# A decoder layer in fp32 on one core: the first norm's weights ride in with x, the other norm weights come later on GpSimd's queue, ten warm-up groups for twelve

## The reference, cut to what matters

```
h    = rmsnorm(x, attn_norm)                     # 16 x 128 weights: the first norm
proj = h @ w_in                                  # queries, keys, values of groups A and B
out_a = dilated_attention(...); out_b = swa_sink_attention(...)
mix  = concat(rmsnorm(out_a, out_norm_a), rmsnorm(out_b, out_norm_b))   # 8 + 8 columns
x    = x + mix @ w_out
h    = rmsnorm(x, ffn_norm)                      # 16 columns
x    = x + (silu(h @ w_gate) * (h @ w_up)) @ w_down
out  = rmsnorm(x, final_norm)
```

## Time and profile before

| | |
|---|---|
| median of 3 runs | 1980.23 us (1979.84 to 1980.58) |
| the profiled execution, whole | 1983.18 us |
| its span, first to last instruction | 1981.4 us |
| PE busy | 1968.1 us (99%) |
| DVE busy | 1654.0 us (83%) |
| ACT busy | 1124.8 us (57%) |
| POOL busy | 165.6 us (8%) |
| DMA, first of 40 slices | 9 tenths busy, 323 GB/s; mean over the span 139 GB/s |

### The profile page before, as it was taken

How to read it: one execution, slowest core, us unless ns; L and a number is a source line. 1 busy time by engine, 2 the same in 40 slices (tenths; PEclk the granted TensorE clock), 3 DMA queues, 4 the chain that set the end, 5 groups by cost and what they waited for, 6 DMA issues and landing times.

```text
span 1981.4 us, 29278 instructions
## 1 busy us (share of the span) xinstructions
PE 1968.1 (99%) x10300; PEld 1691.7 (85%) x10300; DVE 1654.0 (83%) x2384; ACT 1124.8 (57%) x2064; POOL 165.6 (8%) x261
## 2 busy tenths in 40 slices
PE   9999999999999999999999999999999999999998
PEld 7788888888888988888888888888888888888886
DVE  7877777767766999999999999999998688697886
ACT  6566666666446655555555555555556355566643
POOL 4002333323100000000000000000000000000000
PEclk9999999999999999999999999999999999999999
DMA  9422222223334344433434434444446846546433
GB/s 323 143 80 75 65 72 72 70 70 120 118 115 143 118 142 136 139 132 134 138 128 138 136 131 137 138 134 133 137 138 232 304 123 224 177 148 222 126 129 133
DMA packets 132745, 276.16 MB, mean 139 GB/s; under 512 B 13376, under 2 KB 13408, under 8 KB 131600
## 3 DMA queue, kind: packets, MB, share of 16 engines
q1 hardware_dynamic: 120752, 239.65, 37.8%
q0 software_dynamic: 6640, 23.82, 3.1%
q10 hardware_dynamic: 5232, 11.04, 1.6%
HBM read 242.99 MB, written 31.46 MB: 139 GB/s over the span
## 4 chain that ended last, share of the span: by engine, by line
PE 95%; DVE 2%; issue 1%; DMA 1%; ACT 0%; SPq 0%; POOLq 0%; POOL 0%; DVEq 0%; ACTq 0%
PE bank L835 25%; PE bank L838 13%; PE bank L762 7%; PE bank L764 7%; PE bank L763 7%; PE bank L696 7%; PE bank L698 7%; PE bank L697 7%; PE bank L894 3%; PE bank L892 3%; PE bank L893 3%; PE bank L919 2%; PE bank L936 1%; PE bank L904 1%; PE bank L903 1%
## 5 line engine op out<-in xcount | busy, mean ns | idle before, releaser
L835 PE MATMUL bank<-s_two,t_hi 128*128 128x512 f32 x2352 | 557.3, 390 | 0.0
L1479 ACT ACTIVATE t_hi<-t_raw 128x1792 fp32r<-128x1792 f32 x176 | 302.1, 1718 | 358.8 <-DVE t_raw L2149 272.0
L835 PEld LDWEIGHTS bank<-s_two,t_hi 128*128 128x128 f32 x2352 | 433.5, 188 | 84.7
L2155 DVE TENSOR_TENSOR t_lo<-t_raw,t_hi 128x1792 fp32r<-128x1792 f32 x176 | 355.3, 2019 | 22.0 <-ACT t_hi L1479 21.9
L838 PEld LDWEIGHTS bank<-s_two,t_lo 128*128 128x128 f32 x2352 | 298.8, 191 | 10.8 <-DVE t_lo L2155 1.0
L838 PE MATMUL bank<-s_two,t_lo 128*128 128x256 f32 x2352 | 302.1, 283 | 0.8 <-DVE t_lo L2155 0.8
L1130 ACT ACTIVATE w_hi<-raw 128x512 fp32r<-128x512 f32 x268 | 168.4, 629 | 191.5 <-PE bank L764 141.3
L1772 DVE TENSOR_TENSOR w_lo<-raw,w_hi 128x512 fp32r<-128x512 f32 x268 | 184.0, 688 | 58.0 <-ACT w_hi L1130 57.5
L2146 DVE TENSOR_TENSOR t_raw<-t_raw 128x1024 f32<-128x1024 f32 x176 | 214.7, 1220 | 16.7 <-DMA t_raw<-in_w_gu 14.5
L696 PE MATMUL bank<-h_hi,w_hi 128*128 128x512 f32 x416 | 166.1, 399 | 2.5 <-DVE w_lo L1772 1.9
L698 PE MATMUL bank<-h_lo,w_hi 128*128 128x512 f32 x416 | 162.6, 391 | 0.0
(11 more groups left out here) (257 smaller groups left out, 3483.6 us busy)
## 6 DMA issues: line engine op xcount, KB each, us to landing
t_raw<-in_w_gu SPq DMA_DIRECT2D x348, 256.0 KB, 2.8
raw<-in_w_down SPq DMA_DIRECT2D x112, 256.0 KB, 3.5
raw<-in_w_in SPq DMA_DIRECT2D x104, 256.0 KB, 2.7
gu_mid<-part POOLq DMA_DIRECT2D x43, 512.0 KB, 2.9
gu_next<-gu_mid SPq DMA_DIRECT2D x36, 512.0 KB, 6.5
raw<-in_w_out SPq DMA_DIRECT2D x64, 256.0 KB, 3.0
fast_y<-in_w_down SPq DMA_DIRECT2D x24, 512.0 KB, 5.0
fast_z<-in_w_down SPq DMA_DIRECT2D x16, 512.0 KB, 4.7
```

Of the source, the lines that this page charges most:

```text
L835: mm = nc.tensor.matmul(b[:, :], t_hi[r][:, ti, q, :], both, start=d == 0 and q == 0, stop=d == DOUBLES - 1 and q == 1 and i < 4, skip_gro ...
L1479: nc.scalar.activation(t_hi[r][:, :, :, :].rearrange("p a q c -> p (a q c)"), t_raw[r][:, 1:8, :, :].rearrange("p a q c -> p (a q c)"), AC ...
L2155: nc.vector.tensor_tensor(t_lo[r][:, :, :, :].rearrange("p a q c -> p (a q c)"), t_raw[r][:, 1:8, :, :].rearrange("p a q c -> p (a q c)"), ...
```

## The change

The sixteen columns of the first norm are put in front of the first block of x in HBM (`x_head`, 128 rows of 16 + 512 numbers), and the first DMA on SP's queue loads both into one stretch of each partition (`x_head_first`; `gain0` and `x_first` are views of it). `gains` keeps 32 columns; its load moves from ACT's first instruction to POOL's queue, behind `ident` and ahead of `band`. The three waits at the start of ACT, DVE and POOL go; DVE waits for `gains` before `neg_gain`, ACT before its first `act_high`. The warm-up has ten groups instead of twelve. `gains` is 64 bytes shorter in each partition and `gain0` takes 64 bytes ahead of `o_t`, so the tiles in between (`sink` to `h_lo`) stand 64 bytes lower, and so do the later tiles placed by them.

```diff
-WARM = 12
+WARM = 10
...
-    gains = sb("gains", [P, 2 * KD + 2 * PAIRS])
+    gains = sb("gains", [P, KD + 2 * PAIRS])
...
     h_lo = sb("h_lo", [P, KD, SEQ], F32R)
+    spot[0] += KD * BYTES
     place_o = spot[0]
...
-    x_first = sb("x_first", [P, KD, SEQ], at=place_o)
+    x_head_first = sb("x_head_first", [P, KD + KD * SEQ], at=place_o - KD * BYTES)
+    gain0 = x_head_first[:, 0:KD]
+    x_first = x_head_first[:, KD:KD + KD * SEQ].rearrange("p (k c) -> p k c", c=SEQ)
...
-    G_ATTN, G_FFN, G_OUT = 0, KD, 2 * KD
+    G_FFN, G_OUT = 0, KD
...
                 k0, k1 = X_PARTS[m]
+                if m == 0:
+                    sp.dma_start(x_head_first[:, 0:KD + SEQ], x_head).then_inc(x_loaded[0], 16)
+                    continue
...
-                                 scale=gains[:, G_ATTN + k:G_ATTN + k + 1]).then_inc(xt_hi_done, 1)
+                                 scale=gain0[:, k:k + 1]).then_inc(xt_hi_done, 1)
...
                 if p == PAIRS - 1 and s == 3:
+                    act.wait_ge(gains_loaded, 16)
                     act.wait_ge(kb_lo_done, 4)
...
-        act.dma_start(gains[:, :], gain_cols).then_inc(gains_loaded, 16)
         act.wait_ge(ones_done, 2)
         nc.scalar.activation(tick[:, 0:8], half[:, :], ACT.Copy, scale=half[:, 0:1]).then_inc(tables_loaded, 1)
-        act.wait_ge(gains_loaded, 16)
...
-            nc.vector.scalar_tensor_tensor(h_lo[:, k, :], x_first[:, k, :], gains[:, G_ATTN + k:G_ATTN + k + 1],
+            nc.vector.scalar_tensor_tensor(h_lo[:, k, :], x_first[:, k, :], gain0[:, k:k + 1],
...
                 if e == 39:
+                    dve.wait_ge(gains_loaded, 16)
...
-        dve.wait_ge(gains_loaded, 16)
...
-        pool.wait_ge(gains_loaded, 16)
...
-                nc.gpsimd.tensor_scalar(x_first[:, k, :], x_first[:, k, :], gains[:, G_ATTN + k:G_ATTN + k + 1], 1.0,
+                nc.gpsimd.tensor_scalar(x_first[:, k, :], x_first[:, k, :], gain0[:, k:k + 1], 1.0,
...
         nc.gpsimd.dma_start(ident[:, :], c_ident).then_inc(ident_loaded, 16)
+        nc.gpsimd.dma_start(gains[:, :], gain_cols).then_inc(gains_loaded, 16)
```

More of the change, by code:

```diff
@@ L128, with build @@
 HEAD = [("A", 0, 0), ("A", 1, 3), ("B", 0, 6), ("B", 1, 8)]
-def build(nc, x, x_turned, gain_cols, w_in, w_v, sinks, w_out, w_gu, w_down, final_norm, c_dist, c_lnm, c_band, c_slope, c_ident, x_mid, gu_mid, out):
+def build(nc, x, x_head, x_turned, gain_cols, w_in, w_v, sinks, w_out, w_gu, w_down, final_norm, c_dist, c_lnm, c_band, c_slope, c_ident, x_mid, gu_mid, out):
     spot = [(nc.sbuf_base + 63) // 64 * 64]
@@ L2635, in laid_out @@
     x, w_in = np.asarray(inputs["x"]), np.asarray(inputs["w_in"])
-    cols = [np.asarray(inputs[name])[0].reshape(-1, P).T for name in ("attn_norm", "ffn_norm", "out_norm_a", "out_norm_b")]
+    cols = [np.asarray(inputs[name])[0].reshape(-1, P).T for name in ("ffn_norm", "out_norm_a", "out_norm_b")]
+    gain0 = np.asarray(inputs["attn_norm"])[0].reshape(-1, P).T
+    x_head = np.concatenate([gain0, x[0].T[:P]], axis=1)
     w_v = w_in[0][:, 2 * D_A:3 * D_A]
@@ L2641, in laid_out @@
     w_gu = w_gu.transpose(4, 1, 0, 3, 2, 5).reshape(TILES, DOUBLES, 2, P, 4 * P)
-    return {"w_gu": np.ascontiguousarray(w_gu), "x_turned": np.ascontiguousarray(x[0].T), "gain_cols": np.ascontiguousarray(np.concatenate(cols, axis=1)),
+    return {"w_gu": np.ascontiguousarray(w_gu), "x_head": np.ascontiguousarray(x_head), "x_turned": np.ascontiguousarray(x[0].T), "gain_cols": np.ascontiguousarray(np.concatenate(cols, axis=1)),
             "w_in": np.ascontiguousarray(w_in), "w_v": np.ascontiguousarray(w_v)}
```

## The result

| | before | after |
|---|---|---|
| median of 6 runs each | 1980.67 us (1979.84 to 1982.77) | 1989.73 us (1988.95 to 1990.70) |
| profiled execution, span | 1981.4 us | 1988.8 us |
| ratio | | 1.0045 (95% interval 1.0035 to 1.0055) |

A forecast was written before the change was run, and what follows sets the result against it. SyncE's transfers were taken to bound 2 to 54 us, with TensorE 99% busy over the span. 0.10 us less before x's second row and 0.06 more before the fourth gave 0.04 less: 1980.2 us, range 1978.6 to 1982.0.

The forecast's parts named there:

- The step that failed: Tiles moved by 64 bytes: same shapes and operands for each instruction, so zero cost, with no row bounding it otherwise.
- the sign by which it would show: Forecast is wrong if TensorE's instructions from 60 us on take other times, because of the 64 bytes.
- The end moves only with the product at 54.26 us: From 54.26 us on TensorE waits for nothing of the head, so the end moves with that product alone.
- the 1927.1 us behind it: From the product at 54.26 us to the end: the same 1927.1 us expected after the change.
- The wait at 54.26: TensorE's 1.9 us wait, ending on x loads: expected again at another size, with 54.26 moved by less than 1.5 us.
- the second cover that I gave the head: What the head gains in compute is waited away at 39.80 and again at 54.26 us, where the wait was 1.9 us.
- `gains` out of the head: Start of the kernel: first `h_hi` at most 0.29 us earlier, first product 0.1 to 0.3 us earlier.
- The run's start: TensorE's unbroken run, starting at 7.59 us before, would start at about 7.5 us.
- The bytes on POOL's queue: The later `gains` load crosses x's fourth row: 0.06 us; rival, 1.1 us if it behaves like `sink`, chance 0.12.
- The warm-up: Two groups fewer before the first product: costs nothing and gives nothing; its 20 matmuls over by 5.3 us.
- The rival of the clock: Ten groups could put off the rise to 2.4 GHz; decides at 13.8 us at 1.2 GHz, 1984.2 us; chance 0.05.
- something unseen: Remaining case for any cause not named anywhere in the kernel; chance 0.03.

The follow-up runs named there:

- Experiment 2: Kernel before with only the small tile `sink` moved behind `h_lo`, so the tiles between stand 64 bytes lower: 1989.69 us, ratio 1.0046.
- experiment 4: Kernel after with `slope` and `sink` moved behind `h_lo`, so the low tiles stand 256 bytes lower than before against the rest: 1980.91 us, ratio 1.0002.
- experiment 6: Not the layer: bare products at seventeen pairs of operand offsets, other engines still; 512 columns took 226.7 ns at (0, 0), 233.3 at (64, 0).
- experiment 11: Not the layer: bare products again, in another order of blocks; short ones at 64 right behind products at distance 0 ran at 117.8 ns.
- experiment 1: Kernel before with ten warm-up groups instead of twelve and nothing else: 1980.52 us, ratio 1.0003.
- experiment 3: Kernel before with `sink` moved to the top of memory, every tile behind its old place 64 bytes lower, distances between large tiles kept: 1980.15 us, ratio 0.9998.
- experiment 7: The kernel of experiment 4 with twelve warm-up groups instead of ten: 1981.22 us, ratio 1.0002.
- experiment 10: The bare products of experiment 6 with both tiles 224 bytes higher: all seventeen pairs as there within 0.1 ns.

## Why the prediction was wrong, by its own steps

**The step that failed** is the shortest: "The tiles moved by 64 bytes: each instruction has the same shape and the same operands. Zero, and no row bounds it otherwise." That is the whole difference. Experiment 2 has only this and shows +9.1 us, experiment 4 has everything but this and shows +0.3, each against the kernel before on its own chip. I had named the sign by which it would show ("PE's instructions from 60 us on take other times") and had looked at no pair of tiles. The step could have been worked out as far as a question. In the kernel before, the large tiles lie multiples of 256 bytes apart, and so does each pair of them that PE multiplies; the change takes 64 from the tiles up to `h_lo` and leaves those from `o_t` on, so some pairs are no longer so. Which ones:

| products (512 columns if not said) | distance after, modulo 256 | before, ns | after, ns |
|---|---|---|---|
| `h_hi`, `w_hi`: both moved | 0 | 227 | 227 |
| `act_hi`, `w_hi`: the output projection, 530 to 590 us | 64 | 227 | 233 |
| `f_hi`, `a_hi`: down, 1620 to 1900 us | 64 | 226 | 233 |
| `w_hi`, `down_hi`, 1465 to 1550 us | 0 | 227 | 227 |
| `w_hi`, `down_hi`, 1620 to 1900 us, between `f` products | 0 | 226 | 232 |
| `s_two`, `t_hi`: gate and up, by slot | 0 or 64 | 228.2 | 229.8 |
| `s_two`, `t_lo` (256 columns), by slot | 0 or 64 | 120.1 | 118.3 |

Each line is a mean from start to start over the records of the group. The last two, 2352 products each, nearly cancel, 3.8 us lost and 4.0 gained. In the down projection the moving tile `f_hi` is the higher one; its products with `a_hi` and `a_lo` take 232.8 and 230.9 ns, more than the 228.9 of that side in experiment 6, which is there the pace of a long block once it has settled. The fifth was a riddle until experiment 11: these tiles both moved, yet they are slower only behind the `f` products. Split by their place there, the first twelve products behind an `f` product take 230.3 ns on average (500 of them), those further on 226.7 (144); before, all take 226.7. The excess lies in the first ten, as behind the bare (0, 64); the eleventh and twelfth take 226.7. That is 1.8 of the 5.4 us of this stretch: the slow pace outlasts its cause.

The profile's own mean durations hardly show it. The kernel after, by groups from 1620 to 1960 us (line, engine, operation, shapes and count | busy us, mean ns | idle):

```profile
L768 PE MATMUL bank<-w_hi,down_hi 128*128 128x512 f32 x248 | 97.7, 394 | 0.0
...
L769 PE MATMUL bank<-w_lo,down_hi 128*128 128x512 f32 x248 | 96.5, 389 | 0.0
```

Before, all such groups stand at 389. A mean of 394 for 389 ns, 1.3%, and no idle time: this is what nine microseconds look like.

**The end moves only with the product at 54.26 us.** True of the change's own work: that same product starts at 51.35 us in experiment 4 and at 51.27 and 51.32 in experiments 1 and 3, which have the head's loads of before. False of the end, since the 1927.1 us behind it, taken as fixed, grew by 10.0.

**The wait at 54.26.** Forecast to stay, at some other size. It was gone, and not by the change: ACT's fourth square started at 46.06 in the profiled execution of before; after, it reads

```profile
35.74 1.92 ACT L1372 ACTIVATE x_row<-x_row 128x2048 f32<-128x2048 f32 x1 [1.50 <-DMA x_row<-in_x]
...
43.19 1.90 ACT L1372 ACTIVATE x_row<-x_row 128x2048 f32<-128x2048 f32 x1
```

and experiments 1 and 3, whose loads are those of before, have it at 43.04 and 43.01. In the nine other profiled executions of the layer PE waits 0.3 us at this product once and otherwise not at all. The 1.9 us belonged to that one execution, which lay 2.95 us above the median; I had seen that and still took its waits for the kernel's. So the second cover that I gave the head, the wait behind 54 us, wasn't there. It did no harm to the sum: experiments 1, 4 and 7 show nothing gained or lost.

**`gains` out of the head**: the first `h_hi` 0.29 us earlier at most, measured 0.31; the first product 0.1 to 0.3, measured 0.40 (5.68 for 6.08); x0's load took 2.8 us for 2.9, so the rows of 2112 bytes cost nothing that shows. **The run's start**: 7.5, measured 7.42. **The bytes on POOL's queue**: 0.06 us with an upper end of 1.1; no run shows them, and experiment 4 bounds the whole of the change's work by its interval, −1.4 to +2.2 us. **The warm-up**: zero, and experiments 1 and 7 bear it out. One detail of it was off. The 20 matmuls were over at 5.63, not by 5.3, and the first product ran 0.60 us from its successor, the next 0.38:

```profile
0.99 4.64 PE L1056 MATMUL bank<-ones 128*128 128x128 f32 x20 [0.99 <-POOL half L2565]
5.68 0.79 PE L702 MATMUL bank<-h_hi,w_hi 128*128 128x512 f32 x1
6.28 0.55 PE L703 MATMUL bank<-h_hi,w_lo 128*128 128x512 f32 x1
6.66 0.39 PE L704 MATMUL bank<-h_lo,w_hi 128*128 128x512 f32 x1
7.42 0.50 PE L702 MATMUL bank<-h_hi,w_hi 128*128 128x512 f32 x1 [0.37 <-DVE h_lo L1781]
```

The warm-up's matmuls are 0.21 us apart to the end, for 0.11 after the rise in the kernel before, and the third product is the first at the 0.39 us of those from 8 us on (2.4 GHz): the rise from 1.2 to 2.4 GHz came after 6.28 here, at least 1 us later than before, in the first products and not in the warm-up. The second block waited for `h_lo` all the same. The rival of the clock is thus seen at a small size, and it costs nothing. Nor is it the ten groups that put the rise off: in experiment 1, also with ten, the warm-up's matmuls are 0.11 us apart from 3.9 us on, and in experiment 3, with twelve, they are 0.21 apart to the end and the first product, at 6.13, still takes 0.69 us. The rise comes at another moment in each execution.

**The chances.** 3 in 100 for "something unseen" was too little for an edit that moves a good part of the tiles and of which I had written that no row bounds it.

## What to carry to other kernels

An edit that resizes a small tile moves every tile behind it. Before counting it as nothing, list for each kind of matmul the distance of its stationary from its moving tile modulo 256 bytes, before and after; and place the small tiles so that all of them stay (here 192 bytes of small tiles moved behind `h_lo` gave back 8.8 us). This is measured for fp32r products alone, and short ones were faster off distance 0. When a full stretch holds fewer matmuls at the same clock, compare the start-to-start time by pair of tiles; busy shares and waits will not show it. And where the profiled execution lies above the median, look for its excess before trusting its largest wait.

## What the runs showed of the hardware

The time of an fp32r product depends on where its two operands lie to each other in a partition: from 226.7 ns for 512 columns at a distance of 0 modulo 256 bytes, up to 234.4 elsewhere; for 256 columns 120.0 at 0, and 113.3 to 119.9 elsewhere (experiment 6). Both moved together, by 64 bytes (experiment 3) or 224 (experiment 10), changes nothing. The Trainium skill (SBUF — State Buffer, "Who interferes with whom") gives PE two read ports, one for the moving operand and one for weight loads, independent of each other; experiment 6, with the other engines still, shows a product's time change by 6.6 ns of 226.7 with the distance between just these two operands, so their reads are not independent in time, and the measurement decides. How they meet inside the chip isn't shown.

The pace has a memory: a product of 512 columns at distance 0 takes 226.7 ns, or 224 to 241 when it is one of the first six to ten behind products at 64 (experiment 11, and the down projection of the kernel after), and a short product at 64 takes 113.4 or 117.8 through a long series. Why, what chooses between the last two, and why (0, 320) is slower than (0, 64) was not found; nor was a version tried in which all three slots of `t_lo` lie off by 64.

When TensorE's clock rises differs from one execution of the layer to the next: the warm-up's gaps halve at 3.9 us in experiment 1, at 5.2 in the kernel before, and in the kernel after and experiment 3 not before 6 us.
